# Staging rooms, instruction order and SiLU's place in the FFN of a hybrid decoder step

## What is computed

```
hn = rmsnorm(h, ffn_norm_g)
h = h + (jax.nn.silu(hn @ w_ffn_gate) * (hn @ w_ffn_up)) @ w_ffn_down
```

## Time and profile before

| | us |
|---|---|
| median of three runs | 1916.06 (1913.25 to 1920.07) |
| the profiled execution | 1916.04 |
| its span, first to last instruction | 1914.4 |
| TensorE matmul busy | 1786.3 (93%) |
| VectorE busy | 1192.1 (62%) |
| ScalarE busy | 737.0 (39%) |
| FFN, first to last matmul | 1001.4 to 1760.7 |

### The profile page before, as it was taken

The page is one execution under the profiler, slowest core; times in us unless marked ns, Lnnn a source line. Parts: engine busy times, 40 slices in busy tenths (PEclk is TensorE's granted clock), DMA queues, the critical chain, the costliest instruction groups (busy, mean ns, idle before and its releaser), DMA issues. The chain is left out here.

```text
span 1914.4 us, 35497 instructions
## 1 busy us (share of the span) xinstructions
PE 1786.3 (93%) x13062; PEld 1649.2 (86%) x13062; DVE 1192.1 (62%) x1945; ACT 737.0 (39%) x1417; POOL 337.0 (18%) x360
## 2 busy tenths in 40 slices
PE   6999999986999999987998999999999899998998
PEld 6999999884676666766898999999999898988897
DVE  4224733475777777764448776667766868689543
ACT  5114322653655656542324332223332334244320
POOL 1112321001233333342112111111111000000110
PEclk9999999898999999998999999999999999999999
DMA  4323541319999999974111222222222323232121
GB/s 161 104 79 80 150 126 56 91 51 288 320 339 358 342 363 354 337 238 145 45 33 56 68 73 86 68 72 75 69 80 94 123 87 116 73 104 74 56 69 47
DMA packets 232922, 265.72 MB, mean 139 GB/s; under 512 B 16162, under 2 KB 173428, under 8 KB 232756
## 3 DMA queue, kind: packets, MB, share of 16 engines
q1 hardware_dynamic: 211988, 195.36, 32.6%
q0 software_dynamic: 20768, 68.17, 10.6%
HBM read 229.79 MB, written 29.21 MB: 135 GB/s over the span
## 5 line engine op out<-in xcount | busy, mean ns | idle before, releaser
L2508 PE MATMUL psum<-x_second_hi,unit_hi 128*128 128x364 f32 x924 | 305.7, 331 | 13.6 <-DVE x_second_lo L2523 8.5
L2508 PE MATMUL psum<-x_second_hi,unit_lo 128*128 128x364 f32 x924 | 304.5, 330 | 0.0
L2508 PE MATMUL psum<-x_second_lo,unit_hi 128*128 128x364 f32 x924 | 304.4, 329 | 0.0
L150 PE MATMUL psum<-x_hi,w_hi 128*128 128x364 f32 x768 | 183.0, 347 | 9.1 <-DVE x_lo L2222 5.8
L1303 POOL DMA_DIRECT2D dec_v<-in_cache_v x256 | 138.0, 539 | 291.1 <-issue 285.5
L2508 PEld LDWEIGHTS psum<-x_second_hi,unit_hi 128*128 128x128 f32 x924 | 174.8, 189 | 16.2 <-issue 10.3
L2508 PE MATMUL psum<-x_first_hi,unit_hi 128*128 128x364 f32 x528 | 177.1, 335 | 9.5 <-DVE x_first_lo L2523 6.5
L2508 PE MATMUL psum<-x_first_hi,unit_lo 128*128 128x364 f32 x528 | 175.9, 333 | 0.0
L2508 PE MATMUL psum<-x_first_lo,unit_hi 128*128 128x364 f32 x528 | 175.8, 333 | 0.0
L2508 PEld LDWEIGHTS psum<-x_second_hi,unit_lo 128*128 128x128 f32 x924 | 174.7, 189 | 0.0
L2508 PEld LDWEIGHTS psum<-x_second_lo,unit_hi 128*128 128x128 f32 x924 | 174.7, 189 | 0.0
(11 more groups left out here) (310 smaller groups left out, 3321.5 us busy)
## 6 DMA issues: line engine op xcount, KB each, us to landing
dec_k<-in_cache_k SPq DMA_DIRECT2D x256, 256.0 KB, 5.4
dec_v<-in_cache_v POOLq DMA_DIRECT2D x256, 256.0 KB, 5.4
w_raw<-in_w_in SPq DMA_DIRECT2D x25, 512.0 KB, 3.9
scratch_z<-ffn_hidden SPq DMA_DIRECT2D x22, 546.0 KB, 2.8
w_raw<-in_w_ffn_gate SPq DMA_DIRECT2D x22, 512.0 KB, 3.7
w_raw<-in_w_ffn_up SPq DMA_DIRECT2D x22, 512.0 KB, 3.7
w_raw<-in_w_ffn_down SPq DMA_DIRECT2D x16, 512.0 KB, 3.9
feat_swap<-feat_n SPq DMA_DIRECT2D x32, 136.5 KB, 2.4
```

What stands on the lines that cost most here:

```text
L150: ins = pe.matmul(out[:, c, 0:SPAN], w(k), x(k)[:, c * SPAN:c * SPAN + SPAN], start=n == 0 and w is whi and x is xhi, stop=n == len(ks) - ...
L2508: ins = pe.matmul(bank[b], w[unit][:, j, :], x[slot][:, j, :], start=start and j == 0 and w is m.uhi and x is m.xhi7, stop=j == k - 1 and ...
```

## The change

Four things, all in the FFN. The staged inputs `first` and `second` go to the rooms of B21 and B13 instead of B13 and B23, so their loads wait for the fourth and the fifth product instead of the fifth and the sixth; the load of B21 itself goes behind them on SyncE's queue. ScalarE makes the high halves of B13 and B23 in the tile before the group, that of B21 at the group's start. VectorE's order in the tile before a group and in its first tile is written anew: low halves of B13 and B23 come early, `common` of the tile before goes behind the group's first low halves, `bottom_right` and `bottom_left` of both tiles move. And on ScalarE `silu(t-1)` goes behind `copy_p1(t)` in every tile; in tile 22 it goes behind the high halves of X3, X2, X1 and X4 as well, with that of B22 behind it.

```diff
--- before.py
+++ after.py
@@ -1854,7 +1854,7 @@
 TILES = GATE_TILES + len(DOWN_TILES)
 FIRST_OF = [GATE_TILES + g * (KT // 2) for g in range(len(DOWN_GROUPS))]
 X_HI_A = {B23: 6, B21: 7, X3: 8, X2: 9, X4: 10, B22: 11}
-X_HI_B = {B11: 1, B21: 2, B13: 3, B23: 4, X3: 5, X2: 6, X1: 7, X4: 8, B22: 9}
+X_HI_B = {B11: 1, B13: 2, B23: 3, B21: 4, X3: 5, X2: 6, X1: 7, X4: 8, B22: 9}
 X_LO_B = {B11: 1, B13: 2, B23: 3, B21: 4, X3: 5, X2: 6, X1: 7, X4: 8, B22: 9}
 X_HI_FIRST, X_RAW_FIRST = 11, 4
 
@@ -2370,9 +2370,9 @@
                 if 1 <= t <= GATE_TILES:
                     store_z(t - 1)
                 if new:
+                    load_x(2, m.xhif[B21], t, 4, 0, 1)
+                    load_x(4, m.xhif[B13], t, 5, 1, 1)
                     load_x(1, m.xlof[B21], t, 4, 1, 0)
-                    load_x(2, m.xhif[B13], t, 5, 0, 1)
-                    load_x(4, m.xhif[B23], t, 6, 1, 1)
                     load_x(3, m.xlof[B13], t, 5, 0, 2)
                     load_x(5, m.xlof[B23], t, 6, 1, 2)
                 if t + 2 <= TILES:
@@ -2409,7 +2409,7 @@
                 n = {B11: 0, B21: 1, B13: 3, B23: 5, B22: 6}.get(slot)
                 if n is not None:
                     act.wait_ge(x_in[n], 16 * (e + 1))
-                raw = {B13: 3, B23: 1, X3: 1, X2: 2, X1: 3, X4: 4}.get(slot)
+                raw = {B13: 1, B21: 3, X3: 1, X2: 2, X1: 3, X4: 4}.get(slot)
                 if raw is not None:
                     act.wait_ge(s["x_raw"], X_RAW_FIRST + 4 * e + raw)
                 x_hi(slot, m.xlof[slot][:, 0:k, :], k)
@@ -2446,19 +2446,18 @@
             rstd_act(act, m, ps, s)
             for t in range(TILES):
                 new, first = t in before_group, t in FIRST_OF
+                if first:
+                    z_hi(t, B21)
                 if t:
-                    if first:
-                        z_hi(t, B23)
                     unit_hi(act, m, s, t, S4)
-                    if first:
-                        copy_p1(t)
-                    if t <= GATE_TILES:
-                        silu(t - 1)
-                    if not first:
-                        copy_p1(t)
+                    copy_p1(t)
                 if first:
-                    for slot in (X3, X2, X1, X4, B22):
+                    for slot in (X3, X2, X1, X4):
                         z_hi(t, slot)
+                if 1 <= t <= GATE_TILES:
+                    silu(t - 1)
+                if first:
+                    z_hi(t, B22)
                 if FIRST_OF[-1] < t:
                     for n in pair_of(t - 1):
                         square(n)
@@ -2469,13 +2468,12 @@
                 if new:
                     z_hi(t + 1, B11)
                 unit_hi(act, m, s, t + 1, A21)
-                if new:
-                    z_hi(t + 1, B21)
                 unit_hi(act, m, s, t + 1, S3)
                 unit_hi(act, m, s, t + 1, S2)
-                unit_hi(act, m, s, t + 1, S1)
                 if new:
                     z_hi(t + 1, B13)
+                    z_hi(t + 1, B23)
+                unit_hi(act, m, s, t + 1, S1)
                 unit_hi(act, m, s, t + 1, A22)
             for u in range(2):
                 act.wait_ge(ple_w_scaled, u + 1)
@@ -2531,7 +2529,7 @@
                 e, n = epoch(t), half_tiles(t)
                 raw = X_RAW_FIRST + 4 * e
                 done = NPROD * (t - 1)
-                first, second = m.xhif[B13][:, 0:n, :], m.xhif[B23][:, 0:n, :]
+                first, second = m.xhif[B21][:, 0:n, :], m.xhif[B13][:, 0:n, :]
                 b11, b21 = m.xlof[B11][:, 0:n, :], m.xlof[B21][:, 0:n, :]
                 if slot == X3:
                     dve.wait_ge(x_in[2], 16 * (e + 1))
@@ -2663,34 +2661,35 @@
                 new, first = t in before_group, t in FIRST_OF
                 if first:
 
-                    z_lo(t, B23)
                     z_lo(t, B21)
+                    common(t - 1)
                     for unit in (S2, S1, A22):
                         unit_lo(dve, m, s, t, unit)
+                    z_lo(t, X3)
+                    z_lo(t, X2)
                     bottom_right(t - 1)
+                    z_lo(t, X1)
+                    z_lo(t, X4)
                     bottom_left(t - 1)
                 if t:
                     top_right(t - 1)
                     unit_lo(dve, m, s, t, S4)
                     if t <= GATE_TILES and not first:
                         hidden(t - 1)
+                if first:
+                    z_lo(t, B22)
                 third(t)
                 top_left(t)
                 if first:
-                    z_lo(t, X3)
-                    third_of_second(t)
-                    z_lo(t, X2)
-                    z_lo(t, X1)
-                    common(t)
-                    z_lo(t, X4)
-                    z_lo(t, B22)
                     for unit in (A11, A12, A21):
                         unit_lo(dve, m, s, t + 1, unit)
-                    bottom_right(t)
+                    third_of_second(t)
+                    common(t)
                     if t == GATE_TILES:
                         hidden(t - 1)
                     unit_sums(dve, m, s, t + 1)
                     unit_lo(dve, m, s, t + 1, S3)
+                    bottom_right(t)
                     bottom_left(t)
                     for unit in (S2, S1, A22):
                         unit_lo(dve, m, s, t + 1, unit)
@@ -2705,16 +2704,20 @@
                 third_of_second(t)
                 if t < last:
                     unit_lo(dve, m, s, t + 1, A21)
+                if new:
+
+                    z_raw(t + 1, X3)
+                    z_raw(t + 1, X2)
+                    unit_lo(dve, m, s, t + 1, S3)
+                    z_raw(t + 1, X1)
+                    z_lo(t + 1, B11)
+                    z_lo(t + 1, B13)
+                    z_lo(t + 1, B23)
+                    z_raw(t + 1, X4)
+                    continue
+                if t < last:
                     unit_lo(dve, m, s, t + 1, S3)
                 common(t)
-                if new:
-                    z_raw(t + 1, X3)
-                    z_raw(t + 1, X2)
-                    z_raw(t + 1, X1)
-                    z_lo(t + 1, B11)
-                    z_raw(t + 1, X4)
-                    z_lo(t + 1, B13)
-                    continue
                 if t < last:
                     unit_lo(dve, m, s, t + 1, S2)
                 bottom_right(t)
```

More of the change, by code:

```diff
@@ L2707, in _ @@
                     unit_lo(dve, m, s, t + 1, A21)
-                    unit_lo(dve, m, s, t + 1, S3)
-                common(t)
                 if new:
```

## The result

The changed kernel takes 1894.48 us (median of four runs, 1892.9 to 1897.02) against 1915.05 of the kernel before (four runs): 20.6 us less, ratio 0.9895, 95% interval 0.9871 to 0.9918. The forecast was 1898.8, its range 1894.5 to 1905.5, the rival (a) with the quicker load 1896.7. To the forecast's one decimal, the median is the lower end of the range. The forecast started from 1916.0, the median of the three runs of the kernel before; the fourth run brings that median to 1915.05.

The account below looks back on a forecast made before the run. TensorE was taken to bound gate tiles, with losses in tile 1 and three boundaries, whose ends VectorE's queue sets. Gains 7.7 + 3.2 + 3.5 + 2.8 = 17.2 us: 1916.0 - 17.2 = 1898.8 us, range 1894.5 to 1905.5.

Parts of the forecast that it names:

- rival (a): First two boundaries: load undisturbed by those behind it, 4.6 us instead of 5.6, 1.0 each; 1896.7 us, chance 0.12.
- part 1: Tile 1: SiLU behind the copy of p1 removes TensorE's wait and the half clock after it; 7.7 us.
- The cover in the gate tiles: Other 20 gate tiles: `hidden` about 1.1 us later costs nothing, since `third` waits for the third product; 1.2 us of cover.
- part 3: Boundaries: VectorE's queue from X3 to the weight sums sets the end; gains 3.2, 3.5 and 2.8 us.
- B22's wait: Tile 22: VectorE idles 1.9 us because B22's low half stands behind SiLU(21) and B22's high half on ScalarE.
- part 2: Boundaries: new rooms let the second staged input be requested earlier, load 5.6 us; X3 2.0 us sooner, 1.8 at tile 29.
- the requests close behind it: Second staged load: B21's and B13's load close behind the request, so 5.6 us was taken rather than 4.6.
- rival b: Tiles 23, 27 and 31: clock of 0.50 for 3.41 us behind each copy wait loses 1.7 thrice; 1903.9 us, chance 0.10.
- (c): Boundaries only trade waits, the chain over `common`, p1's copy, SiLU and B22 being longer; 1908.3 us, chance 0.10.
- (d): Tile 1 keeps its wait behind something read as early; 1906.5 us, chance 0.04.
- (e): Slower: B23's load blocks ScalarE's queue and delays VectorE's low halves; 1924.6 us at 10 us later, chance 0.03.

Follow-up runs that it names:

- experiment 1: Kernel before with only SiLU moved behind the copy of p1 in the gate tiles; 1909.53 us against 1914.27, ratio 0.9966.
- experiment 3: Changed kernel with both staged inputs requested one product later (fifth and sixth); 1918.08, 1901.43 for the run before and this one, each timed once.
- experiment 4: Changed kernel with `common` of tiles 21, 25 and 29 put back ahead of X3; 1898.51 us, timed once.
- experiment 2: Kernel before with the new rooms, requests and high halves, VectorE's order and SiLU's place as before; 1918.08 us, timed once.
- experiment 6: Changed kernel with B22's high half ahead of SiLU on ScalarE in tile 22; 1893.70 us, timed once.
- experiment 5: Changed kernel with the copy of p1 of tiles 23, 27 and 31 ahead of the weight halves on ScalarE; 1897.06 us, timed once.

## Why the prediction was right

**Tile 1** (part 1): right in size and cause; experiment 1 has the 7.7 alone. The cover in the gate tiles held: `hidden` was said to start at 3.75 and started at 3.71. That VectorE's instruction would be stretched by GpSimd's was wrong in its direction; `hidden` was there first, and GpSimd's scaling took 0.41 longer in tile 20 (1.91 to 2.64 us in tiles 3 to 20), which nobody waits for. Nor was the pair in tile 1 the only one in the trace before: in tiles 3 to 19 each a `unit_lo` that began during the scaling took 1.3 to 1.5 us instead of 0.68. In all these pairs the one that began second was the one stretched. And the fourth product was due at 1034.61, 0.17 later than the prediction has it; the 7.7 stands.

**VectorE's queue** (part 3): 36.1, 34.9 and 28.5 us of work were worked out, 36.08, 34.86 and 28.42 came; the lengths from X3 to the sums, with B22's wait of 1.9, were 38.3, 35.2 and 28.8, and came out at 38.45, 35.33 and 29.38. The 0.58 too much at the third is the two sums' waits for the eighth and ninth product, which the prediction had counted as a later X3. Experiments 3 and 4 show that this queue sets the end, and experiment 2 that the rooms alone don't. But the end does not follow "from VectorE's queue alone": the places of two instructions on ScalarE are in it with 2.0 us (B22's high half, experiment 6) and with 1.0, 0.5 and 0.2 (the copy, experiment 5).

**The load** (part 2) is the term that was mis-sized: 5.6 us were taken for the second staged input, 4.6 were measured, so X3 came at 14.88 and 14.82 us into tiles 21 and 25 instead of 15.8. This 1.0 at two boundaries is the difference between 3.2 + 3.5 and 4.2 + 4.6, and it is rival (a). But the runs do not bear out the reason that the prediction weighed, the requests close behind it. In the six kernels with the new rooms and this place of the request it took 4.6 to 5.9 us at these two boundaries, 5.0 in the mean of twelve, with the same three followers; in the kernel before and in experiment 1, with the next request 2.0 later, the request at this place took 4.6 to 5.2, 5.0 in the mean of four. With the same followers it differs by 1.3 from execution to execution. What makes it vary I did not test. So 5.6 was too much, but that the profile of the changed kernel has 4.6 at both boundaries is luck: with 5.0 it would have gained 0.4 less at each, by the one for one of experiment 3. The Trainium skill (DMA: Bandwidth & Descriptors, Queues, rings and completion order) says that an engine consumes the descriptors of a ring in order; the traces agree in so far as the three followers made no visible difference.

**The clock** (rival b): no row of 0.50 stands in the boundaries of the changed kernel, and in the FFN after tile 0 none at all; the waits there are 1.6 us and less. Before, two rows of 3.41 us stood in the first boundary and one in the second, half of each lost. What such a row costs differs. Experiment 2 has none in its second boundary and is 0.52 shorter there, by just as much as its X3 came earlier: there the row of the kernel before had cost nothing. Experiment 1 has one instead of two in the first boundary and is 1.39 shorter, with X3 0.12 later. So about 1.4 of the 4.2 at the first boundary is a fall of the clock that the old order does not have in every execution. Experiment 4 has a row of 0.50 behind the start of tile 22, and TensorE still waits 1.55 for the copy in tile 23, so it cost nothing there. Nor do the rows stand behind the longest waits alone, as the prediction has it: before, 2.16 us in tile 22 had one and 2.22 in tile 30 had none. The three boundaries together took 208.9 us in the trace of the kernel before, 208.5 in that of experiment 1, and 197.2 in that of the changed kernel.

Rivals (c), (d) and (e) did not happen: B23's high half, the last that waited for a load ahead of the weight halves, ended at 1485.48 on ScalarE, and VectorE came to it at 1486.02. That is 0.5 us of cover where the prediction has 1.4: X3's earlier start used up the rest; with an input quicker by more than that VectorE would wait for this load, which no run here shows.

Of the whole time, 20.6 against 17.2: 19.75 lie in the FFN, 2.55 more than forecast: 2.1 at the two boundaries with the quicker load, 0.3 in tile 0, 0.1 at the third boundary. The 0.8 between 19.75 and the medians' 20.6 is less than the stages ahead of the FFN vary by. The other 1.0 between 1898.8 and 1894.48 is the start from 1916.0 instead of 1915.05.

## What to carry to other kernels

Where two engines hand work back and forth at a boundary, add up the queue of the one that is never idle from the event that starts it; that sum gave the time from X3 to the weight sums within 0.6 us three times, and said beforehand that the new wait of TensorE at tile 22's fourth product would cost nothing (experiment 4). An input that comes earlier is worth little while something else stands ahead of its consumer in the same queue (experiment 2: 1 us instead of 11). Before a wait is removed, look for what stands next behind it: the copy's wait was 1.6 us, and taking it away was worth 1.0 (experiment 5). Compare stretches of the trace when an effect is smaller than what the stages around it vary by.

## What was not expected of the hardware

The same wait may or may not lower TensorE's clock. In tile 30 the kernel before and experiment 1 both waited 2.22 us for X3's low half; in the latter the clock was granted at 0.50 (1.2 GHz) for 3.4 us from 1.0 us behind it on, in the former not, and the third boundary of experiment 1 took 1.39 us more. Experiment 4 has the same within one execution: TensorE waited 2.73 us at the start of tile 22 and 2.74 at the start of tile 26, both times for B11's low half; behind the first the clock fell to 0.50 for 3.41 us, behind the second it stayed at 1.00. What decides it these runs do not show. TensorE on the timeline of tile 30 in the kernel before:

```profile
1702.07 0.41 PE L2508 MATMUL psum<-x_second_hi,unit_hi 128*128 128x364 f32 x1 [2.22 <-DVE x_second_lo L2523]
```

The same in experiment 1:

```profile
1692.73 0.41 PE L2505 MATMUL psum<-x_second_hi,unit_hi 128*128 128x364 f32 x1 [2.22 <-DVE x_second_lo L2520]
```

Busy time behind the wait, columns as above, in the kernel before and then in experiment 1:

```profile
1703.04:1706.44 3.40, 3.40 (x21) 3.22 (x20) 2.49 (x4) 0.00 (x0) 0.00 (x0) 1.00 0.00 0
1693.70:1697.10 3.40, 3.40 (x13) 3.40 (x12) 1.74 (x2) 0.00 (x0) 0.00 (x0) 0.50 0.00 0
```
